# Expert stage of a two-block model: weight tiles made the stationary operand, tokens the moving one

## The reference

```
D_FF = 128 * ((8 * D_MODEL // 3 + 127) // 128)          # 2816
cap = EC_CAPACITY * n_ // N_EXPERTS                      # 66
g, idx = lax.top_k(jnp.swapaxes(aff, 1, 2), cap)
xs = jax.vmap(lambda ub, ib: ub[ib])(u, idx)
hid = (jax.nn.silu(jnp.einsum('becd,edf->becf', xs, w_gate))
       * jnp.einsum('becd,edf->becf', xs, w_up))
y = jnp.einsum('becf,efd->becd', hid, w_down) * g[..., None].astype(h.dtype)
return jnp.zeros_like(h).at[jnp.arange(b_)[:, None, None], idx].add(y)
```

## Time and profile before

| | |
|---|---|
| median of 3 runs | 4336.51 us (4333.21 to 4339.36) |
| span of the profiled execution (from its first to its last instruction; no other time of it is recorded) | 4340.1 us |
| busy: TensorE matmuls, weight loads, VectorE, ScalarE, GpSimd | 92%, 73%, 70%, 53%, 27% |
| expert stage, first to last matmul | 559.5 to 2079.5 us, 1520 us, 95.0 us per expert |

### The profile page before, as it was taken

The page is one execution under the profiler, slowest core; times in us unless marked ns, Lnnn a source line. Parts: engine busy times, 40 slices in busy tenths (PEclk is TensorE's granted clock), DMA queues, the critical chain, the costliest instruction groups (busy, mean ns, idle before and its releaser), DMA issues. The chain is left out here.

```text
span 4340.1 us, 57933 instructions
## 1 busy us (share of the span) xinstructions
PE 4013.6 (92%) x21773; PEld 3172.6 (73%) x21773; DVE 3017.4 (70%) x3710; ACT 2295.9 (53%) x2928; POOL 1193.4 (27%) x555
## 2 busy tenths in 40 slices
PE   7888689999999999999699799688999999999999
PEld 6876556666666666666579777667889999978877
DVE  4364478888888888888446443443699777688885
ACT  3433257677767766776334345322237988333332
POOL 2211200010000001000222231322253555667662
PEclk9998899999999999999799899799999999999999
DMA  3212379999999999999323331323256999999995
GB/s 94 78 55 81 138 280 378 366 376 380 367 367 374 374 367 371 380 355 367 123 90 115 130 102 49 131 71 104 79 193 214 329 346 348 363 353 371 362 360 192
DMA packets 294835, 1082.17 MB, mean 249 GB/s; under 512 B 23186, under 2 KB 163730, under 8 KB 246520
## 3 DMA queue, kind: packets, MB, share of 16 engines
q1 hardware_dynamic: 254088, 936.49, 57.9%
q0 software_dynamic: 40560, 143.16, 9.0%
HBM read 1001.57 MB, written 77.97 MB: 249 GB/s over the span
## 5 line engine op out<-in xcount | busy, mean ns | idle before, releaser
L1757 ACT CAST moe_expert_high<-moe_expert_raw 128x2048 fp32r<-128x2048 f32 x570 | 973.4, 1759 | 387.4 <-DMA moe_expert_raw<-in_w_down_blocks 133.7
L1526 DVE TENSOR_TENSOR moe_expert_low<-moe_expert_raw,moe_expert_high 128x2048 fp32r<-128x2048 f32 x380 | 817.7, 2198 | 171.8 <-ACT moe_expert_high L1757 171.4
L3091 ACT CAST peer_high<-peerbuf_table_raw 128x1024 fp32r<-128x1024 f32 x256 | 255.8, 1048 | 430.0 <-PE peer_ps L3074 277.8
L679 POOL TENSOR_TENSOR branches_proj_low<-branches_proj_raw,branches_proj_high 128x2048 fp32r<-128x2048 f32 (+3 forms) x58 | 247.2, 4262 | 672.3 <-ACT branches_proj_high L659 614.2
L1644 POOL DMA_INDIRECT scratch_h<-ffn_result,ffn_y_rows x16 | 64.0, 4000 | 1232.2 <-DVE ffn_result L1796 1232.2
L1526 DVE TENSOR_TENSOR ffn_expert_low<-moe_expert_raw,moe_expert_high 128x2048 fp32r<-128x2048 f32 (+1 forms) x192 | 362.6, 1930 | 52.2 <-ACT moe_expert_high L1757 51.9
L3045 PE MATMUL peer_ps<-peerbuf_hnT_high,peer_high 128*128 128x384 f32 x1024 | 352.7, 344 | 5.2 <-ACT peer_high L3091 5.2
L2894 DVE TENSOR_TENSOR peer_low<-peerbuf_table_raw,peer_high 128x1024 fp32r<-128x1024 f32 x185 | 262.8, 1449 | 119.9 <-ACT peer_high L3091 119.7
L3046 PE MATMUL peer_ps<-peerbuf_hnT_low,peer_high 128*128 128x384 f32 x1024 | 345.2, 337 | 0.0
L1686 PE MATMUL ffn_gate_p<-moe_expert_high,ffn_x_high 128*66 128x512 f32 (+1 forms) x768 | 284.2, 377 | 1.2 <-DVE ffn_x_low L1826 1.2
L1687 PE MATMUL ffn_gate_p<-moe_expert_high,ffn_x_low 128*66 128x512 f32 (+1 forms) x768 | 283.0, 375 | 0.0
(11 more groups left out here) (551 smaller groups left out, 9379.2 us busy)
## 6 DMA issues: line engine op xcount, KB each, us to landing
moe_expert_raw<-in_w_gate_blocks SPq DMA_DIRECT2D x80, 2048.0 KB, 9.7
moe_expert_raw<-in_w_up_blocks SPq DMA_DIRECT2D x80, 2048.0 KB, 9.2
moe_expert_raw<-in_w_down_blocks SPq DMA_DIRECT2D x80, 2048.0 KB, 9.9
peerbuf_table_raw<-in_peer_down_t SPq DMA_DIRECT2D x64, 1024.0 KB, 7.7
peerbuf_table_raw<-in_peer_up_t SPq DMA_DIRECT2D x64, 1024.0 KB, 8.0
branches_proj_raw<-in_w_in SPq DMA_DIRECT2D x36, 1024.0 KB, 5.4
scratch_a<-peer_gelu SPq DMA_DIRECT2D x64, 384.0 KB, 9.2
scratch_g<-peer_spread SPq DMA_DIRECT2D x24, 1024.0 KB, 14.0
```

Of the source, the lines that this page charges most:

```text
L679: pool.tensor_tensor(owner.slot_of(owner.low, at), owner.slot_of(owner.raw, at), owner.slot_of(owner.high, at).bitcast(F32), ALU.subtract) ...
L1526: return engine.tensor_tensor(self.half_of(self.low, q, h), self.half_of(self.raw, q, h), self.half_of(self.high, q, h).bitcast(F32), ALU. ...
L1757: act.copy(half_of(high, q, h), half_of(raw, q, h)).then_inc(high_done, 1)
L3091: act.copy(high[:, q % 2, cols], raw[:, q % PR_RAW, cols]).then_inc(high_done, 1)
```

## The change

The operands change places. A tile of 128 x 128 weights is now stationary, and the tokens move: `x_pair` holds for each k the 66 columns of x_high and behind them the 66 of x_low, 132 columns together. Each weight tile, first of high and then of low, is multiplied with the pair, so that there are four products where there were three (low by low is new). The sums come out turned, hidden values on partitions and tokens along the free axis, in two halves of 66 columns (from x_high and from x_low) that are added afterwards. The turn of the hidden values is gone; the result of the down product has to be turned back instead.

- Chunks of 384 columns in place of 512: `FF_N` 8 (the last of 128), `FF_NB` 24, a ring of 4 slots. Bytes loaded, cast and subtracted stay the same.
- TensorE: per expert 22 x 8 tiles in each of three matrices, high and low: 1056 matmuls of 132 columns, in place of 372 of 512 and 48 of 256 columns. 22 turns of hidden values go; 8 turns of y come.
- ScalarE and VectorE: per chunk a copy of one half of the gate and the up sums out of PSUM and an addition of the other (`sum`), silu and product from SBUF (`join`), the split of the hidden values (`part`), and the same sum for y.

```diff
-FF_CHUNK = 512
+FF_CHUNK = 384
-FF_RING = 3
+FF_RING = 4
+PAIR = 2 * CAP
...
-                        for k in range(KD):
-                            pe.matmul(out, x_high[:, k, 0:CAP], hi[:, k, :], start=(k == 0), stop=False)
-                            pe.matmul(out, x_low[:, k, 0:CAP], hi[:, k, :], start=False, stop=False)
+                        for f in range(n):
+                            for k in range(KD):
+                                pe.matmul(psum[:, s, f * PAIR:(f + 1) * PAIR], hi[:, k, f * P:(f + 1) * P],
+                                          x_pair[:, k, 0:PAIR], start=(f == 0 and k == 0), stop=False)
                         low_in(q)
-                        for k in range(KD):
-                            last = pe.matmul(out, x_high[:, k, 0:CAP], lo[:, k, :], start=False, stop=(k == KD - 1))
+                        for f in range(n):
+                            for k in range(KD):
+                                last = pe.matmul(psum[:, s, f * PAIR:(f + 1) * PAIR], lo[:, k, f * P:(f + 1) * P],
+                                                 x_pair[:, k, 0:PAIR], start=False, stop=(f == n - 1 and k == KD - 1))
...
-                        for t, cols in parts:
-                            pe.matmul(down_p[:CAP, cols], t_high[:, s, t, 0:CAP], hi[:, t, cols],
-                                      start=(c == 0 and t == 0), stop=False)
-                            pe.matmul(down_p[:CAP, cols], t_low[:, s, t, 0:CAP], hi[:, t, cols], start=False, stop=False)
+                        for t in range(n):
+                            for k in range(KD):
+                                pe.matmul(down_p[:, k // 3, k % 3 * PAIR:(k % 3 + 1) * PAIR], hi[:, t, k * P:(k + 1) * P],
+                                          t_pair[:, c % T_RING, t, 0:PAIR], start=(c == 0 and t == 0 and k % 3 == 0),
+                                          stop=False)
...
+                def turn_y(e, a):
+                    pe.wait_ge(y_summed, 2 * e + 2)
+                    if a == 1:
+                        pe.wait_ge(result_out, 2 * e + 1)
+                    for k in range(KD // 2):
+                        last = pe.transpose(turn_p[:CAP, k * P:(k + 1) * P], y[:, a * KD // 2 + k, :], ident[:, :])
+                    last.then_inc(y_turned, 1)
...
+                            if step == "sum":
                                 act.wait_ge(block_used, used(e, "gate", c))
+                                if c >= 2 or not first:
+                                    act.wait_ge(hidden_done, e * FF_N + c - 1)
+                                act.copy(gate[:, s, 0:n, :], sums(gate_p, c, 1)).then_inc(part_out, 1)
+                                act.wait_ge(block_used, used(e, "up", c))
+                                act.copy(up[:, s, 0:n, :], sums(up_p, c, 1)).then_inc(part_out, 1)
+                            elif step == "join":
+                                act.wait_ge(gate_summed, e * FF_N + c + 1)
+                                act.activation(gate[:, s, 0:n, :], gate[:, s, 0:n, :], ACT.Silu).then_inc(silu_done, 1)
+                            elif step == "part":
                                 act.wait_ge(hidden_done, e * FF_N + c + 1)
-                                act.activation(silu[:, s, 0:width], gate_p[:CAP, s, 0:width], ACT.Silu
-                                               ).then_inc(silu_done, 1)
...
+                                act.copy(t_part(c, 0), hidden[:, s, 0:n, :]).then_inc(t_high_done, 1)
```

More of the change, by code:

```diff
@@ L1554, in expert_ffn @@
         ring.block_of, ring.half_of, ring.raw, ring.high, ring.low, ring.raw_in, ring.high_done, ring.low_done)
+    tail = FF_N - 1
+    y_at = (at[("up", 2)], at[("up", 3)])
+    steps_at = {q: [] for q in range(FF_NB)}
+    for c in range(FF_N):
+        i = at[("up", c)]
+        summed, joined, parted = (i + 3, i + 4, i + 5) if c < tail else (FF_NB - 2, FF_NB - 1, FF_NB - 1)
+        steps_at[summed].append(("sum", c))
+        steps_at[joined].append(("join", c))
+        steps_at[parted].append(("part", c))
+    steps_at[FF_NB - 2].append(("x", 0))
+    steps_at[FF_NB - 1].append(("x", 1))
+    rank = {"part": 0, "join": 1, "sum": 2, "x": 3}
+    for q, steps in steps_at.items():
+        steps.sort(key=lambda s: (s[1] if s[0] != "x" else FF_N, rank[s[0]] if s[1] != tail else -rank[s[0]]))
     with Stage(nc, "ffn") as st:
-        low.append(st.sb("expert_low2", [P, KD * FF_CHUNK], F32R))
+        for q in range(FF_AHEAD, FF_RING):
+            low.append(st.sb(f"expert_low{q}", [P, KD * FF_CHUNK], F32R))
         x_raw = st.sb("x_raw", [CAP, D])
@@ L1592, in x_turned_part @@
         def x_turned_part():
[L1593 to L1612, removed]
+            return turn_p[:, 0:KD // 2 * CAP].rearrange("p (k c) -> p k c", c=CAP)
@@ L1614, in expert_ffn, with y_part @@
+        def y_part(part):
+            return (y[:, 0:6, :].rearrange("p (b f) s -> p b f s", b=2) if part == 0 else
+                    y[:, 6:8, :].rearrange("p (b f) s -> p b f s", b=1))
         with nc.Block() as block:
@@ L1691, in columns @@
                         last.then_inc(block_used, 1)
[L1693 to L1701, removed]
@@ new lines, in down @@
+                        low_in(q)
+                        for t in range(n):
+                            for k in range(KD):
+                                last = pe.matmul(down_p[:, k // 3, k % 3 * PAIR:(k % 3 + 1) * PAIR],
+                                                 lo[:, t, k * P:(k + 1) * P], t_pair[:, c % T_RING, t, 0:PAIR],
+                                                 start=False, stop=(c == tail and t == n - 1 and
+                                                                    (k % 3 == 2 or k == KD - 1)))
@@ L1724, in _ @@
                     for c in range(FF_N):
[L1725 to L1731, removed]
+                        columns("gate", c, gate_p, gate_summed)
+                        columns("up", c, up_p, up_summed)
+                        for a in range(2):
+                            if not first and at[("up", c)] == y_at[a]:
+                                turn_y(e - 1, a)
+                        if c == tail:
+                            if not first:
+                                pe.wait_ge(result_out, 2 * e)
                             turn_x(e + 1, 0)
@@ L1739, in _, with take_down, take_y, take_x @@
                     down(FF_N - 1)
+                turn_x(0, 0)
+                pe.wait_ge(x_low_done, 1)
+                turn_x(0, 1)
+                expert(0, first=True)
+                with pe.Fori(1, EXPERTS) as e:
+                    expert(e)
+                pe.wait_ge(x_low_done, 2 * EXPERTS + 2)
+                turn_y(EXPERTS - 1, 0)
+                turn_y(EXPERTS - 1, 1)
             @block.scalar
             def _(act):
-                act.sem_inc(result_out, 2)
-                def take_result(e):
-                    act.wait_ge(block_used, used(e, "down", FF_N - 1))
+                def take_down(e):
+                    act.wait_ge(block_used, used(e, "down", tail))
+                    for part in range(2):
+                        act.copy(y_part(part), y_sums(part, 1)).then_inc(y_part_out, 1)
+                def take_y(e):
+                    act.wait_ge(y_turned, 2 * e + 1)
                     act.wait_ge(result_free, e + 1)
-                    act.activation(result[:, 0:512], down_p[:CAP, 0:512], ACT.Copy,
+                    act.activation(result[:, 0:512], turn_p[:CAP, :], ACT.Copy,
                                    scale=slot_gate[:, bass.ds(e, 1)]).then_inc(result_out, 1)
+                def take_x(e, a):
+                    act.wait_ge(x_turned, 2 * e + a + 3)
+                    act.copy(x_part(a, 0), x_turned_part()).then_inc(x_high_done, 1)
                 def expert(e, first=False):
@@ L1758, in expert @@
                         if q == FF_RING - 1 and not first:
[L1759 to L1762, removed]
+                            take_down(e - 1)
+                        for step, c in steps_at[q]:
+                            s, n = c % 2, tiles_of(c)
+                            if step == "sum":
                                 act.wait_ge(block_used, used(e, "gate", c))
+                                if c >= 2 or not first:
+                                    act.wait_ge(hidden_done, e * FF_N + c - 1)
[6 more added lines that the diff above has]
+                            elif step == "part":
@@ L1768, in expert @@
                                 take_x(e + 1, c)
[L1769 to L1777, removed]
-                    act.copy(x_part(x_high, a), x_turned_part()).then_inc(x_high_done, 1)
+                        if q == y_at[0] + 4 and not first:
+                            take_y(e - 1)
@@ L1829, in _ @@
+                        if q == y_at[1] + 4 and not first:
+                            take_y(e - 1)
                 take_x(0, 0)
```

140 lines of the change are left out of this document (77 added, 63 removed).

## The result

The changed kernel takes 6508.54 us (median of 4 runs, 6501.09 to 6516.98), the kernel before 4334.86 on the same chip: a ratio of 1.5006, interval 1.4978 to 1.5035. It is slower by half, as forecast (6480), and for the forecast reason: the expert stage runs at clock 0.50 from its first matmul to its last.

The account below looks back on a forecast made before the run. TensorE was taken to set the pace, transfers close behind. 228.8 us per expert x 16 = 3661, less 1520, plus 4, gave +2145 us and a median of 6480, range 4730 to 6690.

Parts of the forecast that it names:

- The price of a pair: Expert stage, TensorE: one 128-column weight load with its 132-column matmul costs 0.112 us at clock 1.00, 0.213 at 0.50.
- The lower bound of 0.068 for the streaming: TensorE: streaming 132 columns alone takes 0.068 us at clock 1.00, extrapolated from matmuls of 512 and 256 columns.
- The estimate from the Trainium skill: TensorE: about 81 ns per load and matmul at 128 columns, giving 85.5 us per expert, less than now.
- the row: Earlier trace: plain float32 loads of 128 columns follow each other at 0.112 us with only 64 columns moving.
- The step that carried the forecast: Expert stage: entered at clock 0.50, the new load-paced stream stays at 0.50 from first tile to last.
- The row it was read from: Earlier trace: two streams of 24 plain float32 matmuls, 64 columns, loads of 128, busy yet staying at clock 0.50.
- The second rival: Expert stage: the clock rises, a pair costs about 0.112 us, 120.7 us per expert, time 4750; chance 0.23.
- The third: Expert stage: narrow fp32r costs like plain float32 in full, 0.224 us at clock 1.00, time 6640; chance 0.18.
- The sum: Per expert 225.2 us of matmuls, 2.6 of turns and 1.0 of waits: 228.8 us, +2145 us in all.
- the term of the waits: TensorE's waits inside an expert: 1.0 us, bounds 0 and 5, against 1.2 us in the kernel before.
- the first case: Expert stage locked at clock 0.50, the forecast: 6480 us, own range 6360 to 6690; chance 0.52.
- the other side's price: TensorE: the load hides, a pair costs 0.068 or 0.081 us, transfers at 90.3 us decide, time 4260; chance 0.05.

Follow-up runs that it names:

- e1: The changed kernel with 20 matmuls of 512 columns on scratch PSUM once, ahead of the first expert: 6306.54 us.
- e6: The changed kernel with the moving operand cut to the 66 columns of the high part, same loads: 6511.06 us in one run.
- e7: The changed kernel with 20 matmuls of 512 columns ahead of every expert and only 66 columns moving: 6556.16 us in one run.
- e4: The changed kernel with only the first 66 columns of each weight tile loaded, 132 columns still moving: 4454.54 us in one run.
- e2: The changed kernel with 20 matmuls of 512 columns ahead of every expert: 4863.12 us, ratio 1.1204.
- e8: The kernel of e1 with TensorE's loop over experts 1 to 15 written out, so its queue never jumps back: 4738.23 us.
- e3: The changed kernel with moving operands padded with zeros from 132 to 248 columns, same matmuls and loads: 4840.49 us in one run.
- e5: The kernel before with chunks of 384 columns, a ring of 4 and a fourth low buffer, operands not exchanged: 4325.71 us, ratio 0.9975.
- e9: The changed kernel with TensorE's loop over experts written out and nothing else: 6474.01 us in one run.

## Why the prediction was right

- **The price of a pair.** Taken as 0.112 at clock 1.00 from loads of another type and 0.213 at 0.50. Measured 0.111 (e1) and 0.213. The 0.45 us for one record in the second was an assumption; it is 0.418 in the changed kernel. That the load sets the price is shown from both sides and at both clocks: half the columns change nothing or little (e6 0.213, e7 0.108), half the load gives 0.115 and 0.063 (e4). The lower bound of 0.068 for the streaming was no bound: behind a load of 66 columns the matmul took 0.063 (e4). The estimate from the Trainium skill (TensorE: Matmul & The Clock Gate, Back-to-back issue gap), 81 ns, was too low for fp32r weights, as the row had said.
- **The clock.** The step that carried the forecast was that a stream paced by loads, entered at 0.50, stays there. This stream stayed for 3690 us. e1, e2 and e8 show that this is a matter of how it is entered: at 1.00 the same instructions stay at 1.00. As a rule the step was too broad. With 248 columns behind the same loads (e3), or 132 behind half a load (e4), the stream entered at 0.50 rose in its first microseconds. With 66 columns it did not even hold 1.00 (e7). The row it was read from had 64 columns, and no row told on which side of it 132 would fall. The chance of 0.52 said as much, and that it came out this way is in part luck. The rule of the Trainium skill that sustained activity releases the throttle (TensorE: Matmul & The Clock Gate, What's actually happening) would have given 4750; no run bears it out for this stream, in which TensorE was busy for 3646.7 of 3690 us at 0.50. It agrees with e3, e4 and the 512-column bursts, where the clock rose.
- **The second rival** (the clock rises) did not come about by itself, but e8 is its kernel: 4738 measured, 4750 worked out. The third, a narrow matmul as dear as a plain one, is excluded by e1, e4 and e5. All three cases lay inside the range of 4730 to 6690, so it is the clock and the distance that single out the first, and not the range.
- **The sum.** 228.8 us per expert were forecast, 3690 / 16 = 230.6 measured. TensorE's busy part is 3646.7 / 16 = 227.9, against 225.2 + 2.6 = 227.8. The difference is the term of the waits: 1.0 was taken, (3690 - 3646.7) / 16 = 2.7 measured, within its bounds of 0 to 5. Nearly all of it, 40.8 of 43.3 us, are the gaps of 2.9 us on average at each jump back, which nothing in the kernel before had shown. 1.7 x 16 = 27 us are nearly all of the 28.5 by which the forecast fell short. A slip: with 0.221 a pair and 5 us of waits the upper end of the first case is 6676 and not 6690.
- **Hidden work.** VectorE was put at 89 us per expert and took 1385 / 16 = 86.6, ScalarE at 76 and took 71.9. The transfers stood at 0.42, where about 0.4 was written.
- **What was wrong in a rival:** the other side's price. In e4, which has half of the load, TensorE waits for the gather of the tokens and the kernel takes 4454 us. By that, even a hidden load would not have made the exchange faster as it stands.

Left open: why the jump back costs 1.7 to 3.6 us here and shows no such gap in the kernel before, whose loop body has 450 matmuls instead of 1072. The instruction queue moves 4.59 MB in the changed kernel, 1.98 before and 4.15 without jumps, which fits a body that has to be fetched again at each jump, but no run varied the size of the body. Open too is what decides whether such a gap costs the clock (e2).

## What to carry to other kernels

Before operands change places, put the load's time beside the streaming time of one matmul: at clock 1.00 a pair with a full 128 x 128 load of fp32r weights cost 0.111 us with 132 moving columns, 0.114 with 248 and 0.120 with 256. Fewer columns than that leave TensorE waiting for loads while the profile shows it fully busy. Then look at PEclk where the stage is entered, because such a stream may not lift it: this one kept whichever clock it found, until a gap. The loss of 2174 us falls into three parts. The clock was 1736 (e9 6474.0 against e8 4738.2, which differ by one burst of wide matmuls), the gaps at the jumps were 34.5, and the remaining 403 are what e8 loses against the kernel before (4738.2 against 4334.9), the dearer pair at clock 1.00. If such a stream must be, enter it behind wide matmuls and leave no gap of microseconds in it, and check that the clock row stays at 1.00.

## What the runs showed of the hardware

- The same instructions ran for a whole stage at either clock, 3690 us at 0.50 and 1910 us at 1.00, by what stood ahead of them (changed kernel, e8).
- With 132 columns behind each load the clock once given was kept over 1900 us (e8); with 66 it was lost in each expert some 4.4 us after the stream began (e7), with TensorE's loads busy throughout. With 248 columns, or with 132 and half of the load, a clock of 0.50 was lifted within the first 48 matmuls (e3, e4).
- An idle time of 2.28 us at the head of an expert was enough to lose it (e1). In e2 seven such gaps cost it and seven did not: one of 1.72 us did, one of 2.29 did not.
- Adding work made it faster: 248 columns in place of 132 took 4840 us in place of 6508 (e3).
